# Hybrid decoder block: weights read in place or packed block by block, input packed tile by tile, and another order of the first loads

## What is computed

```python
h = rmsnorm(x, norm_mix_g)
proj = h @ w_in                      # (2048, 6664)
aq, ak, av, mq, mk, mv, mo, mi, mf = split(proj)
attn = dilated_attention(aq, ak, av) # 12 heads of 128: q/k norm, rotary, 3 dilations
qk = silu(causal_conv4(mq | mk))
hm = rmsnorm(mlstm(qk, mv, mi, mf) * sigmoid(mo))   # 4 heads, chunks of 128
x = x + concat(attn, hm) @ w_out     # (2048, 2048)
h2 = rmsnorm(x, norm_ffn_g)
gate, val = split(causal_conv3(h2 @ w_up))          # (2048, 2*5632)
x = x + (silu(gate) * val) @ w_down  # (5632, 2048)
```

## Time and profile before

| | us |
|---|---|
| median of 3 runs | 3471.54 |
| lowest, highest of them | 3468.32, 3572.19 |
| the profiled execution | 3468.32 |
| its span, slowest core (core 3) | 3467.3 |
| its span, fastest core (core 0) | 3433.8 |

### The profile page before, as it was taken

The page is one execution under the profiler, slowest core; times in us unless marked ns, Lnnn a source line. Parts: engine busy times, 40 slices in busy tenths (PEclk is TensorE's granted clock), DMA queues, the critical chain, the costliest instruction groups (busy, mean ns, idle before and its releaser), DMA issues.

```text
span 3467.3 us, 43781 instructions; the slowest of 8 cores (3433.8 to 3467.3 us)
## 1 busy us (share of the span) xinstructions
PE 3122.8 (90%) x16028; PEld 1484.6 (43%) x16028; DVE 1557.3 (45%) x2184; ACT 1066.0 (31%) x1698; POOL 52.8 (2%) x102
## 2 busy tenths in 40 slices
PE   3796888788878786899999999999999999999999
PEld 1342444344444443344444444444444444444444
DVE  2445343365655554111666666600036666663000
ACT  1334644355555554233222222200012222221000
POOL 0000000000000000000000000000000000000000
PEclk9898999999999998899999999999999999999999
DMA  8221122320222025666433333476653344434564
GB/s 184 74 49 25 33 57 60 96 57 10 59 59 59 13 55 154 173 169 154 86 77 74 73 73 73 93 160 128 135 123 74 73 79 83 82 74 84 123 139 110
DMA packets 134227, 308.12 MB, mean 89 GB/s; under 512 B 18944, under 2 KB 88576, under 8 KB 122112
## 3 DMA queue, kind: packets, MB, share of 16 engines
q0 software_dynamic: 16032, 174.99, 27.3%
q1 hardware_dynamic: 117984, 130.34, 13.0%
HBM read 427.85 MB, written 52.43 MB: 139 GB/s over the span
## 4 chain that ended last, share of the span: by engine, by line
PE 79%; ACT 7%; DVE 5%; DMA 5%; issue 4%; SPq 0%; ACTq 0%; DVEq 0%
PE ps L926 35%; PE ps L967 18%; PE ps L658 9%; PE ps L872 5%; PE ps L487 3%; DVE mem L421 2%; DMA x1d<-mem 2%; PE ps L363 2%; PE ps L473 2%; DMA mem<-xT 1%; PE ps L736 1%; ACT mem L765 1%; ACT mem L665 1%; PE ps L738 1%; DMA mixd<-mem 1%
## 5 line engine op out<-in xcount | busy, mean ns | idle before, releaser
L926 PE MATMUL ps<-mem,wslot 128*128 128x512 bf16 x5632 | 1216.1, 379 | 0.0
L926 PEld LDWEIGHTS ps<-mem,wslot 128*128 128x128 bf16 x5632 | 551.1, 98 | 664.5
L967 PE MATMUL ps<-mem,wslot 128*128 128x512 bf16 x2816 | 608.1, 379 | 0.0
L944 DVE SCALAR_TENSOR_TENSOR mem<-mem,cfs 128x1024 f32<-128x1024 f32 x352 | 452.1, 1284 | 289.1 <-ACT mem L941 204.3
L941 ACT ACTIVATE mem<-mem,cfs 128x1024 f32<-128x1024 f32 x176 | 217.0, 1233 | 752.8 <-DVE mem L933 752.5
L967 PEld LDWEIGHTS ps<-mem,wslot 128*128 128x128 bf16 x2816 | 275.5, 98 | 332.2
L658 PE MATMUL ps<-mem,wslot 128*128 128x512 bf16 x1536 | 367.4, 395 | 0.7 <-ACT mem L492 0.7
L933 DVE TENSOR_TENSOR mem<-ps,mem 128x512 f32<-128x512 f32 x352 | 243.0, 690 | 131.3 <-PE ps L926 110.5
L976 DVE TENSOR_TENSOR mem<-ps,mem 128x512 f32<-128x512 f32 x64 | 44.3, 692 | 553.1 <-PE ps L967 546.2
L872 PE MATMUL ps<-mem,wslot 128*128 128x512 bf16 x1024 | 241.0, 390 | 4.9 <-DVE mem L748 4.9
L658 PEld LDWEIGHTS ps<-mem,wslot 128*128 128x128 bf16 x1536 | 155.7, 101 | 188.4 <-issue 30.5
(11 more groups left out here) (117 smaller groups left out, 2316.0 us busy)
## 6 DMA issues: line engine op xcount, KB each, us to landing
wslot<-wa POOLq DMA_DIRECT2D x60, 2048.0 KB, 13.2
wslot<-wb POOLq DMA_DIRECT2D x32, 1408.0 KB, 10.9
mem<-xT SPq DMA_DIRECT2D x8, 2048.0 KB, 14.7
mem<-xT SPq DMA_DIRECT2D x64, 256.0 KB, 4.8
x1d<-mem SPq DMA_DIRECT2D x64, 256.0 KB, 3.5
mem<-x1d SPq DMA_DIRECT2D x64, 256.0 KB, 9.3
outT<-mem SPq DMA_DIRECT2D x64, 256.0 KB, 4.0
mixd<-mem SPq DMA_DIRECT2D x64, 128.0 KB, 1.8
```

The costliest lines, as they stand in the source:

```text
L926: K.mm([lambda e, kc=kc: e.matmul(ps[bi][:], sl[:, kc, c0:c0 + 128], h2p[:, kc, t2 * TT:(t2 + 1) * TT], start=(kc == 0), stop=(kc == KC - ...
L944: K.op(dve, lambda e, k=k: e.scalar_tensor_tensor(out=a, in0=y[:, k:k + HS], scalar=wc(k), in1=a, op0=ALU.mult, op1=ALU.add), [B_yy, B_cf, ...
L967: K.mm([lambda e, k=k: e.matmul(ps[bi][:], slv[:, k, jc2 * 128:(jc2 + 1) * 128], actT[:, kh * 22 + k, t2 * TT:(t2 + 1) * TT], start=(kh == ...
```

## The change

Five parts:

1. The weights are read from `w_in`, `w_out`, `w_up` and `w_down` as they are. A block is a rectangle of 512 columns (rows of 2 KB in HBM), or two rectangles or one of 256 columns (rows of 1 KB): 16 rows on each partition for 512 columns, 32 for two of 256, 22 for a block of `w_down`. `_pack` goes.
2. The input is stored tile by tile, `xt`: for each tile of 256 positions 16 KB in one row on each partition. `xload` takes its 512 positions from two tiles, in two rows of 1 KB. `wg` is stored in rows of 512 bytes.
3. The first tile is loaded in four DMAs with semaphores of their own, and squared and summed in four quarters.
4. The second weight block is issued in `norm_a(3)`, after POOL has waited for input tile 5, and `cb` in `norm_a(7)`; before, both were issued at the start.
5. PE starts with 150 matmuls of the matrix of ones with itself, into a PSUM bank that the second norm overwrites.

```diff
-    xT = nc.dram_tensor("xT", [D, S], F32, kind="ExternalInput").ap()
-    wa = nc.dram_tensor("wa", [39, P, 8192], F32, kind="ExternalInput").ap()
-    wb = nc.dram_tensor("wb", [16, P, 5632], F32, kind="ExternalInput").ap()
-    w_g = nc.dram_tensor("w_g", [D, 8], F32, kind="ExternalInput").ap()
+    xt = nc.dram_tensor("xt", [S // 256, P, KC * 256], F32, kind="ExternalInput").ap()
+    wgd = nc.dram_tensor("wgd", [P, KC * 8], F32, kind="ExternalInput").ap()
+    w_in = nc.dram_tensor("w_in", [D, INW], F32, kind="ExternalInput").ap()
...
+    w_in_v = w_in.rearrange("(kc p) n -> p kc n", p=P)
...
+    xt_v = xt.rearrange("t p (k n) -> p t k n", n=256)
...
-    blocks = [(wa[i], 8192) for i in range(17)]
+    for c0 in (5632, 4608, 5120, 6144, 3072, 3584, 4096):
+        if not blocks:
+            blocks.append([(lambda s, q=q: wv(s)[:, 4 * q:4 * q + 4, :], w_in_v[:, 4 * q:4 * q + 4, c0:c0 + 512])
+                           for q in range(4)])
+        else:
+            blocks.append([(wv, w_in_v[:, :, c0:c0 + 512])])
...
     for hf in range(2):
-        blocks += [(wa[17 + i], 8192) for i in range(22)] + [(wb[i], 5632) for i in range(16)]
+        for ub in range(22):
+            blocks.append([(lambda s: s[:].rearrange("p (k n) -> p k n", n=512)[:, :, 0:256],
+                            w_up_v[:, :, ub * 256:(ub + 1) * 256]),
+                           (lambda s: s[:].rearrange("p (k n) -> p k n", n=512)[:, :, 256:512],
+                            w_up_v[:, :, DFF + ub * 256:DFF + (ub + 1) * 256])])
...
-        src, n = blocks[i]
-        cuts = range(0, n, n // 4 if i == 0 else n)
-        w = n // len(cuts)
-        K.dma(pool, [wslots[sl][:, c:c + w] for c in cuts], [src[:, c:c + w] for c in cuts], B_ws[sl], True)
+        K.dma(pool, [vf(wslots[sl]) for vf, src in blocks[i]], [src for vf, src in blocks[i]], B_ws[sl], True)
...
-        K.dma(sp, xs[tt % 3], xT_v[:, :, tt * TA:(tt + 1) * TA], B_xs[tt % 3], True)
-
-    xin(0)
+        K.dma(sp, xs[tt % 3], xt_v[:, tt, :, :], B_xs[tt % 3], True)
+
+    for q in range(4):
+        K.dma(sp, xs[0][:, 4 * q:4 * q + 4, :], xt_v[:, 0, 4 * q:4 * q + 4, :], B_xq[q], True)
     K.dma(sp, cf[:], cfd, B_cf, True)
     xin(1)
     xin(2)
     w_issue()
-    K.dma(pool, wg[:], w_g.rearrange("(kc p) n -> p kc n", p=P), B_wg, True)
-    w_issue()
-    K.dma(pool, cb[:], cbd, B_cb, True)
+    K.dma(pool, wg[:].rearrange("p k n -> p (k n)"), wgd, B_wg, True)
+    K.mm([lambda e: e.matmul(ps[7][:, 0:128], ones, ones, start=True, stop=True)] * 150, [B_one], [B_ps[7]])
...
-        K.op(act, lambda e: e.activation(out=sq, in_=x_t, func=AF.Square), [B_x], [B_sq])
-        K.mm([lambda e, kc=kc: e.matmul(pb[:, 0:TA], ones, sq[:, kc, :], start=(kc == 0), stop=(kc == KC - 1))
-              for kc in range(KC)], [B_sq, B_one], [B_pb])
+        npc = 4 if tt == 0 else 1
+        for q in range(npc):
+            ks = range(q * KC // npc, (q + 1) * KC // npc)
+            K.op(act, lambda e: e.activation(out=sq[:, ks[0]:ks[-1] + 1, :], in_=x_t[:, ks[0]:ks[-1] + 1, :], func=AF.Square),
+                 [B_xq[q] if tt == 0 else B_x], [B_sq])
+            K.mm([lambda e, kc=kc: e.matmul(pb[:, 0:TA], ones, sq[:, kc, :], start=(kc == 0), stop=(kc == KC - 1))
+                  for kc in ks], [B_sq, B_one], [B_pb])
...
         if tt + 3 < NTA:
             xin(tt + 3)
+        if tt == 3:
+            pool.wait(B_xs[2].w)
+            w_issue()
+        if tt == NTA - 1:
+            K.dma(pool, cb[:], cbd, B_cb, True)
...
-            K.dma(sp, xr[i % 8], xT[jc * 128:(jc + 1) * 128, T * TT:(T + 1) * TT], B_xr[i % 8], True)
+            K.dma(sp, xr[i % 8].rearrange("p (t n) -> p t n", n=256), xt_v[:, 2 * T:2 * T + 2, jc, :], B_xr[i % 8], True)
```

More of the change, by code:

```diff
@@ L187, in build @@
     dbg = stage != "FULL"
-    xT = nc.dram_tensor("xT", [D, S], F32, kind="ExternalInput").ap()
-    wa = nc.dram_tensor("wa", [39, P, 8192], F32, kind="ExternalInput").ap()
-    wb = nc.dram_tensor("wb", [16, P, 5632], F32, kind="ExternalInput").ap()
-    w_g = nc.dram_tensor("w_g", [D, 8], F32, kind="ExternalInput").ap()
+    xt = nc.dram_tensor("xt", [S // 256, P, KC * 256], F32, kind="ExternalInput").ap()
+    wgd = nc.dram_tensor("wgd", [P, KC * 8], F32, kind="ExternalInput").ap()
+    w_in = nc.dram_tensor("w_in", [D, INW], F32, kind="ExternalInput").ap()
+    w_out = nc.dram_tensor("w_out", [D, D], F32, kind="ExternalInput").ap()
+    w_up = nc.dram_tensor("w_up", [D, 2 * DFF], F32, kind="ExternalInput").ap()
+    w_down = nc.dram_tensor("w_down", [DFF, D], F32, kind="ExternalInput").ap()
     cbd = nc.dram_tensor("cb", [P, NCB], F32, kind="ExternalInput").ap()
@@ L200, in build @@
     h2d = nc.dram_tensor("h2d", [D, S // 2], BF16, kind="ExternalOutput" if dbg else "Internal").ap()
-    xT_v = xT.rearrange("(kc p) t -> p kc t", p=P)
+    w_in_v = w_in.rearrange("(kc p) n -> p kc n", p=P)
+    w_out_v = w_out.rearrange("(kc p) n -> p kc n", p=P)
+    w_up_v = w_up.rearrange("(kc p) n -> p kc n", p=P)
+    w_down_v = w_down.rearrange("(kc p) n -> p kc n", p=P)
+    xt_v = xt.rearrange("t p (k n) -> p t k n", n=256)
     h2d_v = h2d.rearrange("(kc p) t -> p kc t", p=P)
@@ L243, in build @@
     triu = cf[:, CF_TRIU:CF_TRIU + 128]
+    blocks = []
     wv = lambda s: s[:].rearrange("p (k n) -> p k n", n=512)
-    blocks = [(wa[i], 8192) for i in range(17)]
-    for hf in range(2):
-        blocks += [(wa[17 + i], 8192) for i in range(22)] + [(wb[i], 5632) for i in range(16)]
+    for c0 in (5632, 4608, 5120, 6144, 3072, 3584, 4096):
[4 more added lines that the diff above has]
+            blocks.append([(wv, w_in_v[:, :, c0:c0 + 512])])
+    for hp in range(NHA // 2):
+        blocks.append([(lambda s, i=i: wv(s)[:, :, i * 256:(i + 1) * 256], w_in_v[:, :, c0:c0 + 256])
+                       for i, c0 in enumerate([hp * 256, 1536 + hp * 256])])
+    for jb in range(4):
+        blocks.append([(lambda s: s[:].rearrange("p (k n) -> p k n", n=512), w_out_v[:, :, jb * 512:(jb + 1) * 512])])
+    for hf in range(2):
+        for ub in range(22):
[3 more added lines that the diff above has]
+                            w_up_v[:, :, DFF + ub * 256:DFF + (ub + 1) * 256])])
+        for jb2 in range(8):
+            for kh in range(2):
+                blocks.append([(lambda s: s[:, 0:22 * 256].rearrange("p (k n) -> p k n", n=256),
+                                w_down_v[:, kh * 22:(kh + 1) * 22, jb2 * 256:(jb2 + 1) * 256])])
     wstate = {"issued": 0, "used": 0}
@@ L329, in build @@
     mvt = mvt.rearrange("p (c n) -> p c n", n=512)
+    B_xq = [K.buf("xq%d" % q) for q in range(4)]
     def xin(tt):
-        K.dma(sp, xs[tt % 3], xT_v[:, :, tt * TA:(tt + 1) * TA], B_xs[tt % 3], True)
-    xin(0)
+        K.dma(sp, xs[tt % 3], xt_v[:, tt, :, :], B_xs[tt % 3], True)
+    for q in range(4):
+        K.dma(sp, xs[0][:, 4 * q:4 * q + 4, :], xt_v[:, 0, 4 * q:4 * q + 4, :], B_xq[q], True)
     K.dma(sp, cf[:], cfd, B_cf, True)
@@ L1033, in _params @@
     return cfn
[L1035 to L1053, removed]
 _NC_CACHE = {}
@@ L1063, in run @@
     cfn = _params(inp)
-    w_in = inp["w_in"][0]
-    wan, wbn = _pack(w_in, inp["w_out"][0], inp["w_up"][0], inp["w_down"][0])
+    w_in = np.ascontiguousarray(inp["w_in"][0])
+    w_out = np.ascontiguousarray(inp["w_out"][0])
+    w_up = np.ascontiguousarray(inp["w_up"][0])
+    w_down = np.ascontiguousarray(inp["w_down"][0])
+    wgn = np.ascontiguousarray(w_in[:, 6656:].reshape(KC, P, 8).transpose(1, 0, 2).reshape(P, KC * 8))
     in_maps = []
     for b in range(ncores):
-        in_maps.append({"xT": np.ascontiguousarray(inp["x"][b].T), "wa": wan, "wb": wbn, "w_g": np.ascontiguousarray(w_in[:, 6656:]), "cb": cbn, "cf": cfn, "cs": cs})
+        in_maps.append({"xt": np.ascontiguousarray(inp["x"][b].reshape(8, 256, KC, P).transpose(0, 3, 2, 1).reshape(8, P, KC * 256)), "wgd": wgn,
+                        "w_in": w_in, "w_out": w_out, "w_up": w_up,
+                        "w_down": w_down, "cb": cbn, "cf": cfn, "cs": cs})
     res = run_bass_kernel_spmd(nc, in_maps, core_ids=list(range(ncores)))
```

## The result

| | before | after |
|---|---|---|
| median beside each other, 4 runs each | 3472.29 | 3451.85 |
| ratio, 95% interval | | 0.9941 (0.9919 to 0.9964) |
| the profiled execution | 3468.32 | 3448.01 |
| its slowest core | 3467.3 (core 3) | 3447.0 (core 1) |

The change is worth 20 us, 0.6%. Forecast were 3416 us and a range of 3394 to 3446: the kernel is faster, but by little more than a third of what was forecast, and the time lies above the range.

What follows compares the result with a forecast made beforehand. PE was taken to idle on DMA at the start, cs and output projection. Core 3: 3467.3 - 16 - 10 - 28 = 3413; core 5: 3415, plus 1.0 around it, forecast 3416 us, range 3394 to 3446.

Steps and rivals of the forecast that it cites:

- the queues take one row each in turn: DMA engines shared by POOL's and SP's queues: one row from each in turn, whatever its length, so long rows get most bandwidth.
- Rival 1: DMA queues: turns longer than a row, short weight rows starve SP as long ones do; 3447 us, chance 0.12.
- the start: Before the first projection matmul: long input rows and held-back loads bring it to 47 us, 16 us earlier (9 to 23).
- the 150 matmuls cost nothing: Warm-up on PE at the start: at most 17 us, hidden beside the load of the first input tile.
- the output projection: Stores to x1d no longer wait behind long weight rows: 28 us less on core 3, some 18 on core 5.
- the `mixd` wait: Output projection, core 3: the fourth PE wait, 13.0 us, comes behind mixd loads on SP's own queue and stays.
- All other weight blocks ... stay hidden, at nothing.: Up and down projections: short-row blocks still land within POOL's waits of up to 27.5 and 18.5 us; cost nothing.
- rival 3: Up and down projections wait for weights because short rows are dearer, deciding from 100 or 97 ns a row; 3604, chance 0.08.
- cs: Load of the cos/sin table: lands at about 664.5 us, taking 10 of 13.3 us of PE idle (bounds 0 and 15).
- the slowest core was sought among cores 3 and 5 alone: Final sum: core 3 at 3413 and core 5 at 3415 us, so the slowest is about 3415.

Runs made afterwards that it cites:

- e4: The kernel before with only the input stored by tiles and loaded in 16 KB rows; first projection matmul at 41.4 us, mean span 3451.8 us.
- e8: The changed kernel without the 150 matmuls at the start; the start took 47.4 us.
- e1: The changed kernel with the two h2 reloads moved behind the third and fourth column pairs of the down projection; mean span 3444.4 us.
- e2: The changed kernel with w_up and w_down packed again in long rows; mean span 3426.8 us.
- e5: The kernel before with only the q/k and w_out blocks read in place; mean span on cores 0 to 3 3434.9 us.
- e9: The changed kernel with only w_down packed again in long rows; mean span 3421.3 us.
- e10: The changed kernel without the two loads that bring h2 back for the second half; mean span 3424.8 us.
- e11: The changed kernel with w_up and w_down packed except the first two w_up blocks, and input tiles from the second in 2 KB rows; 3420.82 us, ratio 0.9866.
- e3: The changed kernel with the second weight block and cb issued at the start again; mean span 3442.8 us.

## Why the prediction was wrong, and where it was right

**Right: the queues take one row each in turn, from 1 to 32 KB.** 163 to 160 packets with rows of 16 against 2 KB, 1796 to 1800 with 2 against 2 KB. Rival 1, longer turns that starve SP, falls, since the waits behind the stores went. The rule of the Trainium skill (DMA: Bandwidth & Descriptors, "Queues, rings and completion order"), 9 to 17 descriptors a turn, doesn't agree with this case's trace. The waits alone don't decide that: the prediction let the weights take so many rows in a turn but the store only one, and by the rule for both queues the 8 rows of a store could have gone in one turn. The single packets of before decide it, which follow each other row by row. For the tiny rows of `wg` it holds against 1 KB and is open against 16 KB (e4).

**Right: the start**, -15.8 us as a mean against -16 forecast, at 46.1 on core 3 against 47; and that the 150 matmuls cost nothing (e8). That it came so near is in part luck: the same first loads took 51.1 and 51.3 in e1 and e2. **Right: the output projection**, -30.0 on core 3 against -28, -22.4 on core 5 (275.6 to 253.2) against -18, with the `mixd` wait the one that stays. On core 3 the waits gave 23.6 of it, where 23.3 was forecast, and PE's busy time, now more often at the fast clock, 6.5 against 4.5. e2 and e5 give each half of its cause a price.

**Wrong, the largest: "All other weight blocks ... stay hidden, at nothing."** Two things were wrong in that step. The cost of a `w_down` block was that of its rows by themselves, 8.4 to 16.0 us, and not of a row and its turn. From 2222 to 2226 us 547 weight rows passed 16 engines, 4 x 16 / 547 = 117 ns each with SP's row between, over the 97 from which rival 3 decided; alone, from 2234 on, it is 4 x 16 / 1551 = 41. 176 rows at 117 ns are 20.6 us, and no weight row passed in the first 5.0 us after the issue, where 2 were allowed: 25.6 us, where PE wanted the block after 18.2. It landed after 27.3, since the 16 engines weren't done together (from 22.6 to 27.3 us after the issue) and the last one counts. And the room was read by the kind of the block that loads, where it is that of the block that PE works on meanwhile: the first `w_up` block of the second half has 18.4 us and not 27.6.

Rival 3 had the mechanism and even named SP's traffic, but put it at all 76 blocks or none. It holds where SP has a long queue of short rows of its own: at the reload. That, the late `w_up` block at the second seam and the smaller waits away from them cost 14.4 us as a mean, 12.3 on core 3, 18.7 on core 1. Of core 1's 18.7, 15.0 are its two waits; the rest goes with 13.7 us at 1.2 GHz in these stages, where there was none before.

**Wrong in size: cs, -10.** PE's wait fell by 6.4 on core 3 and by 4.6 as a mean, and the attention without half its time at 1.2 GHz by 3.7 (673.3 to 669.6). On core 1 cs was issued at 639.07 and used at 652.95, 13.9 us later, where 10.5 was forecast (654 to 664.5): a store issued just ahead of it passed its first row only 3.2 us after its issue, from 641 to 644 the queue still carried 400 rows of that store beside 892 weight rows, and cs itself took some 9 us. In the run shown the clock took more back than that, 69.6 against 56.9 us at 1.2 GHz, which is worth 6.4. e1, e2, e9 and e10, with the same code up to the end of the attention, had 61.2, 57.2, 58.5 and 62.0, and an attention of 698.8 to 701.0 us: that the attention of after is 2.6 us longer than before is peculiar to that run.

**Wrong: the slowest core was sought among cores 3 and 5 alone.** They had most to win at the output projection and won it. Core 1 won 12.4 there and lost 18.7 behind.

Core 3's sum shows the sizes. Forecast 54 us less, measured 36.8: 12.3 lost in the up and down projections and 11.1 at the attention (+1.1 where -10 stood; 7.0 us more at 1.2 GHz make 3.5 of it), against 2.7 more won at the start and output projection and 3.5 in the stages between; 12.3 + 11.1 - 2.7 - 3.5 = 17.2.

**Not settled:** why the `w_up` block at the second seam is as late as it is. It was issued at 2505.49 on core 1 and needed 23.7 us, where a block by itself (issued at 1905.87) needed 16.0, and it had 18.4. SP had 720 rows from 2505 to 2530 us, 45 for each engine. At the 91 ns of a 2 KB row their turns make 4.1 us, an estimate: that brings 16.0 to 20.1, past the room of 18.4, and leaves 3.6 us open. Long rows remove the wait (e2, e11).

## What to carry to other kernels

Where two queues share the DMA engines by rows, the length of a row is a priority: give the longer rows to the transfer that must win in that stage, and the shorter to the one with room, stage by stage and not for a whole tensor (e11). A transfer that is hidden in the steady state is to be priced again at every seam, with a row of the other queue ahead of each of its own, and against the time that the engine works on the block before it. And the slowest of eight cores is worked out for all eight.

## What the runs showed that was not expected

- Holding the second block and cb back was worth nothing that shows (e3): the start took 51.3 us without it, 47.2 to 51.3 with it.
- A load of 2048 tiny rows that nobody looks at held up PE by 3.8 to 20.3 us, by core, once its neighbour on the other queue got 16 KB rows (e4).
- In every version and on every core the attention is, to within some 5 us, as long as a constant plus half of its time at 1.2 GHz: the mean of that constant is 673.3 before and 673.8 in e4, and 668.6 to 670.7 in the versions with short q/k blocks that were read over all cores. That time at 1.2 GHz ranged from 57 to 70 us between runs of the same code, 6 us of length, more than the 3.7 that cs gave.
